# Second layer's latent keys: copy of the values, scaling of the keys and fetch of two weights, moved

## Chip, cores and metric

One Trainium2 chip, one core. The metric is the device time of one launch in microseconds (us). Before the change it was 4139.23 us, median of 3 runs (4138.19 to 4139.9).

## What is computed

The reference is a chain of two blocks over 1024 tokens of width 1024: a hybrid layer (multiscale pooling, an RWKV-7 scan, a mixture of experts) and then two attention layers, the first with grouped queries, the second with latent keys and values ("MLA"). All is float32. The change touches the second attention layer alone, and there the building of keys and values:

```python
MLA_HEADS = 16; MLA_NOPE = 64; MLA_ROPE = 32; MLA_V = 64; MLA_Q_LORA = 384; MLA_KV_LORA = 256

def kv_heads(kv_a, k_r, n):
    kv = (rms_norm(kv_a, p["kv_a_norm"]) @ p["w_kv_b"]).reshape(B, n, MLA_HEADS, MLA_NOPE + MLA_V)
    k_nope, v = jnp.split(kv, [MLA_NOPE], axis=-1)
    return rms_norm(k_nope, p["k_nope_norm"]), rms_norm(k_r, p["k_rope_norm"]), v
...
kn_all = jnp.concatenate([kc_nope, k_nope], axis=1)   # 256 context + 1024 tokens
v_all = jnp.concatenate([vc, v], axis=1)
o = sweep_query_blocks(lambda qn, qr: mla_attend(qn, qr, kn_all, kr_all, v_all), q_nope, q_rope)
```

## The kernel before

Every engine has its own instruction stream, written by walking one list of steps: `walk(order, *engines)` calls, for each step in the list, one function per engine (PE, ACT, DVE, POOL, SP), and each of them emits its part of the step with its waits on semaphores. So the order of the steps in the list is the order of the instructions on each engine; an instruction that waits holds up all that stands behind it on its engine.

The tokens are 10 tiles of 128 rows (`NTT` = 10: `CTX` = 2 tiles of context, then 8 of the sequence).

**Latents** (`latents`, L2840 on; its list is `order(i)`). For each tile: the product for the keys' latent (step `kv`, L2896), its RMS norm and scaling, the same for the queries' latent (`qa`, L2905), the gate (`gate`, L2916, 16 matmuls of 128x512, evacuated by ACT's `silu` L2965), and `latturn`, the turning of the scaled latents: 2 transposes for keys (L2923) and 3 for queries (L2930) into banks 6 and 7, copied out by DVE (L2981, into `kvaT`) and ACT (L2945, into `qaT`). The turning of tile i-1 stands behind the product of tile i; the last, `latturn` of tile 9, stood alone behind the list. Two steps of the list are fetches on SP's queue: `weights2` at tile 3 (the gate row and four blocks of the output weights, L3063 and L3065) and `weights3` at tile 9, which waits for the last product, turning and evacuations and then fetches the first half of the key and value weights (`sp_load_wk`, L2830, 1024 KB into `wkb`) and of the query weights (`sp_load_wq`, L2834, 1152 KB into `wqb`).

**Keys** (`keys(hh)`, L3133, run for each half `hh` of the 16 heads, 8 heads at a time). For each tile c:

- `key` (L3166): 4 matmuls of 128x512 give keys and values of 8 heads in two banks: 0 and 1 for even c, 2 and 3 for odd c. It waits for the weights, for `kvaT`, and for these banks to be free. In the trace each of these float32 matmuls is two records, so a `key` is "x8".
- `ksquare` (L3244, ACT): squares of the keys, from PSUM. `ksum` (L3297 reduce and L1821 mean on DVE, then the root, L1825, on POOL).
- `kscale`: DVE multiplies the keys by the root (L3306, the one that reads PSUM) and then by the norm's weight (L3309); POOL copies the rotary part beside them (L3373).
- `vcopy` (L3251, ACT): copies the values out of PSUM. It frees the two banks for the `key` of tile c+2.
- `kturn` (L3177): 8 transposes of the scaled keys into banks 4 and 6, copied into `kT` by DVE (L3291, four heads) and ACT (L3236, four heads).

The list, for tile c: `key(c)`, `kturn(c-2)` with both copies, `kscale(c-1)`, `vcopy(c-1)`, `ksquare(c)`, `ksum(c)`, then three slots for the queries of the first block (`mmq` L3187 with its copy `qe` L3316 into and out of bank 5, then `qsquare`, `qsum`, `qscale`, `qnorm`, `qadd`). `vcopy(c-1)` waits for L3306 of the same tile (the token `t["ksrc"]`). After the loop come `kturn(8)`, `kscale(9)`, the first turning of the queries (L3196) and `kturn(9)`; then the attention of this half begins with the scores (L3225).

Of the kernel before, what the change touches and what calls it, by code (L numbers as in the profile page):

```python
# [1804 lines left out]
NTT = CTX + NT  # L1805
# [1032 lines left out]
def latents(k, a, dr, m, mod):  # L2838
# [21 lines left out]
    def order(i):  # L2860

        yield ("kv", i)
        if i:
            yield ("latturn", i - 1)
        yield from (("kvsquare", i), ("kvscale", i), ("krsquare", i), ("krscale", i))
        if i >= CTX:
            yield from (("qa", i), ("kradd", i), ("qasquare", i), ("qascale", i))
        if i and i + 1 < NTT:
            yield ("turn", i + 1)
        if i + 3 < NTT:  # L2870
            yield ("load", i + 3)
        if i and i + 2 < NTT:
            yield from (("square", i + 2), ("mean", i + 2), ("divide", i + 2))
        if i == 3:
            yield ("weights2",)
        if i >= CTX:
            yield ("gate", i)
            if i == NTT - 1:
                yield ("weights3",)
            yield ("silu", i)  # L2880
# [87 lines left out]
    def dve_latents(kind, i=None):  # L2968
# [10 lines left out]
        elif kind == "latturn":  # L2979
            dve.wait_ge(*t["kvturn"])  # L2980
            dve.e.tensor_copy(kvaT[:, :, P * i:P * i + P], k.bank(6)[:, 0:256].rearrange("p (k t) -> p k t", k=2)).then_inc(*evac_v.up())  # L2981
            t["kva"] = free[6] = evac_v.at
        elif kind == "kvsquare":
# [59 lines left out]
    def sp_latents(kind, i=None):  # L3043
# [17 lines left out]
        elif kind == "weights2":  # L3061
            sp.wait_ge(*product.at)
            sp.e.dma_start(m.gate, dr["mod"][1, 0, 2 * D:3 * D].partition_broadcast(P)).then_inc(*m.gates_in.up(16))  # L3063
            for kk in range(4):
                sp.e.dma_start(m.wo[kk], m.wo_v[kk]).then_inc(*m.o_in.up(16))  # L3065
        elif kind == "weights3":
            for tok in (product.at, feed.turned.at, feed.squared.at, feed.t["v", NTT - 1], feed.t["a", NTT - 1]):
                sp.wait_ge(*tok)
            t["wk", 0] = m.sp_load_wk(0)
# [6 lines left out]
def mla(k, a, dr, out, m, programs):  # L3076
# [11 lines left out]
    for i in range(CTX, NTT):  # L3088
        walk(m.order(i), *programs)
    walk([("latturn", NTT - 1)], *programs)  # L3090


# [45 lines left out]
    def keys(hh):  # L3138
        bg = queries(hh, 0)
        for c in range(NTT):  # L3140
            yield ("key", hh, c)
            if c > 1:
                yield ("kturn", c - 2)
            if c:
                yield from (("kscale", c - 1), ("vcopy", c - 1))
            yield from (("ksquare", c), ("ksum", c))
            for _ in range(3):
# [3 lines left out]
        yield ("kturn", NTT - 2)  # L3151
        yield from (("kscale", NTT - 1), ("vcopy", NTT - 1))
        yield from (s for s in bg if s)
        yield from (s for s in q_turn(hh, 0, 0) if s)
        yield ("kturn", NTT - 1)

    def pe_program(kind, *x):
        if kind == "key":
            hh, c = x
            pe.wait_ge(*t["wk", hh])  # L3160
            pe.wait_ge(*t["kva"])
            for half in range(2):
# [67 lines left out]
    def act_program(kind, *x):  # L3230
        if kind == "kturn":
            c = x[0]
# [13 lines left out]
        elif kind == "vcopy":  # L3246
            c = x[0]
            act.wait_ge(*t["ksrc"])
            for tok in t["kT free"]:
                act.wait_ge(*tok)  # L3250
            act.e.activation(V[:, c, :].rearrange("p (h d) -> p h d", h=8), key_source(c)[:, :, 64:128], ACT.Copy).then_inc(*evac_a.up())  # L3251
            t["v"] = free[2 * (c % 2)] = free[2 * (c % 2) + 1] = evac_a.at
        elif kind == "qTe" and x[2]:
# [31 lines left out]
    def dve_program(kind, *x):  # L3285
        if kind == "kturn":
            c = x[0]
# [13 lines left out]
        elif kind == "kscale":  # L3301
            c = x[0]
            dst, r8_ = k8s[c % 2][:, :, 0:64], mx[:, 8 * (c % 2):8 * (c % 2) + 8]
            dve.wait_ge(*t["kroot", c])
            dve.wait_ge(*t["kfree", c % 2])
            dve.e.tensor_tensor(dst, key_source(c)[:, :, 0:64], bc(r8_, 2, 64), ALU.mult).then_inc(*keyed.up())  # L3306
            t["ksrc"] = keyed.at
            dve.wait_ge(*keyed.at)
# [275 lines left out]
```

## Time and profile before

| | |
|---|---|
| median of 3 runs | 4139.23 us (4138.19 to 4139.9) |
| profiled execution | 4141.4 us, its span 4139.7 us |
| mean granted clock of TensorE | 0.965 of full speed |
| PE busy | 3769.9 us (91%) |
| DVE, ACT, POOL busy | 1604.3 us (39%), 1216.1 us (29%), 525.6 us (13%) |
| share of the chain that ended last | PE 78%, DVE 9%, issue 5%, ACT 3%, POOL 2%, DMA 2% |
| L3166 (keys), share of that chain | 2% |

Times in the rows are us from the start of the span. The chain that ended last is followed back from the last instruction; what stands in it is what the end waited for. Matmuls overlap their weight loads and one another, so the duration of one record is longer than the distance to the next.

### The profile page before, as it was taken

What the parts mean: (1) busy time and instruction counts of PE and PEld (TensorE: products, weight loads), DVE (VectorE), ACT (ScalarE), POOL (GpSimd) and SP (SyncE); (2) the same over time, 40 slices, a digit from 0 to 9 for tenths busy, and PEclk for the clock granted to TensorE, in tenths of its full rate; (3) what the DMA queues carried; (4) which work ended last, traced back from release to release, by engine and by line L of the source; (5) the groups of instructions that cost most, each with busy time, mean ns of one, the idle gap of its engine ahead of it and who ended that gap; (6) DMA issues with size and microseconds to landing.
All of it is one profiled execution on the core that took longest, in us unless ns stands there. A gap on an engine that the chain in (4) does not pass through costs nothing.

```text
span 4139.7 us, 56854 instructions
## 1 busy us (share of the span) xinstructions
PE 3769.9 (91%) x24715; PEld 2347.9 (57%) x24715; DVE 1604.3 (39%) x2422; ACT 1216.1 (29%) x2101; POOL 525.6 (13%) x499
## 2 busy tenths in 40 slices
PE   8899999989799999988998988888997999889989
PEld 4466666665477776344555555555553666456654
DVE  2444444443311111823444444443223444444430
ACT  1333323310111111523333333332112444344430
POOL 0211212111000000411100100010112000200001
PEclk9999999999799999999999999998999999999999
DMA  3000000212699999920000000020100000000002
GB/s 105 16 17 22 17 17 12 84 37 102 247 366 365 368 366 337 380 56 16 16 11 6 16 16 16 11 88 28 51 11 32 1 1 12 1 1 1 1 31 72
DMA packets 108048, 346.80 MB, mean 84 GB/s; under 512 B 13350, under 2 KB 39270, under 8 KB 89622
## 3 DMA queue, kind: packets, MB, share of 16 engines
q1 hardware_dynamic: 85862, 284.85, 19.0%
q0 software_dynamic: 9072, 33.03, 2.3%
q10 hardware_dynamic: 12864, 25.27, 1.7%
q8 instruction: 195, 3.19, 0.3%
q14 instruction: 55, 0.45, 0.0%
HBM read 296.94 MB, written 46.19 MB: 83 GB/s over the span
## 4 chain that ended last, share of the span: by engine, by line
PE 78%; DVE 9%; issue 5%; ACT 3%; POOL 2%; DMA 2%; SPq 0%; POOLq 0%; ACTq 0%; DVEq 0%
PE ps L2522 10%; PE ps L1613 8%; PE ps L2018 8%; PE ps L383 7%; PE ps L3225 6%; PE ps L2540 4%; PE ps L2045 4%; PE ps L1630 4%; PE ps L2916 3%; PE ps L1207 3%; DVE sb L1992 2%; PE ps L3166 2%; PE ps L3187 2%; PE ps L457 2%; PE ps L468 1%
## 5 line engine op out<-in xcount | busy, mean ns | idle before, releaser
L2522 PE MATMUL ps<-sb 128*128 128x512 f32 x960 | 472.8, 610 | 55.4 <-DVE sb L2682 22.1
L2018 PEld LDWEIGHTS ps<-sb 128*128 128x128 f32 x2624 | 300.5, 145 | 341.1 <-ACT sb L2026 130.8
L2026 ACT ACTIVATE sb<-ps 128x512 f32<-128x512 f32 x400 | 238.8, 597 | 799.7 <-PE ps L2018 799.7
L2018 PE MATMUL ps<-sb 128*128 128x128 f32 x2624 | 430.1, 288 | 47.7 <-ACT sb L2002 18.5
L2002 ACT ACTIVATE sb<-ps,sb 128x1280 f32<-128x1280 f32 (+1 forms) x288 | 352.1, 1230 | 143.9 <-DVE sb L1995 141.0
L383 PE MATMUL ps<-sb 128*128 128x512 f32 x704 | 356.5, 622 | 5.0 <-DMA sb<-in_w_in 3.4
L1613 PE MATMUL ps<-sb 128*128 128x256 f32 x1504 | 341.6, 380 | 0.8 <-ACT sb L1645 0.8
L3225 PE MATMUL ps<-sb 96*128 96x512 f32 (+1 forms) x768 | 339.5, 536 | 0.0
L2033 DVE COPY sb<-ps 128x512 f32<-128x512 f32 x256 | 177.0, 692 | 413.5 <-PE ps L2018 413.2
L2045 PEld LDWEIGHTS ps<-sb 128*64 128x64 f32 x5248 | 290.2, 139 | 72.5 <-ACT sb L2026 37.0
L2045 PE MATMUL ps<-sb 128*64 128x128 f32 x5248 | 325.7, 279 | 2.9 <-DVE sb L2033 1.6
L1613 PEld LDWEIGHTS ps<-sb 128*128 128x128 f32 x1504 | 283.3, 191 | 57.1 <-issue 22.7
L1992 DVE TENSOR_REDUCE sb<-ps 128x1 f32<-128x1024 f32 (+1 forms) x192 | 200.6, 1046 | 235.3 <-PE ps L3225 231.3
L1983 DVE TENSOR_REDUCE sb<-ps 128x2 f32<-128x2560 f32 (+1 forms) x80 | 191.8, 2398 | 231.9 <-PE ps L2540 231.9
L1825 POOL TENSOR_TENSOR sb<-sb 128x1 f32<-128x1 f32 (+3 forms) x114 | 132.7, 1166 | 1153.4 <-DVE sb L1821 1153.3
L2522 PEld LDWEIGHTS ps<-sb 128*128 128x128 f32 x960 | 163.9, 194 | 174.9 <-issue 105.9
L2540 PE MATMUL ps<-sb 64*128 64x256 f32 (+1 forms) x832 | 183.5, 573 | 4.5 <-ACT sb L2002 2.7
L383 PEld LDWEIGHTS ps<-sb 128*128 128x128 f32 x704 | 120.5, 192 | 107.3 <-issue 99.4
L1630 PE MATMUL ps<-sb 128*128 128x512 f32 x376 | 169.5, 593 | 0.0
L2540 PEld LDWEIGHTS ps<-sb 64*128 64x128 f32 x832 | 104.5, 204 | 105.5 <-issue 94.3
L3225 PEld LDWEIGHTS ps<-sb 96*128 96x128 f32 x768 | 124.4, 195 | 14.3 <-issue 11.5
L961 POOL TENSOR_TENSOR sb<-sb 128x512 f32<-128x512 f32 x72 | 92.3, 1289 | 297.2 <-ACT sb L645 126.5
(361 smaller groups left out, 4677.9 us busy)
## 6 DMA issues: line engine op xcount, KB each, us to landing
sb<-in_exp_gate SPq DMA_DIRECT2D x47, 1024.0 KB
sb<-in_exp_up SPq DMA_DIRECT2D x47, 1024.0 KB
sb<-in_exp_down SPq DMA_DIRECT2D x47, 1024.0 KB
sb<-in_l_w_mod ACTq DMA_DIRECT2D x12, 2048.0 KB
d_ys<-sb SPq DMA_DIRECT2D x47, 512.0 KB, 14.1
sb<-d_x SPq DMA_DIRECT2D x32, 512.0 KB, 4.1
sb<-in_w_in SPq DMA_DIRECT2D x22, 512.0 KB, 4.2
sb<-in_x SPq DMA_DIRECT2D x16, 512.0 KB, 5.0
```

Of the source, the lines that this page charges most:

```text
L383: ins = pe.e.matmul(k.bank(6 + half), wt[i % 2][:, kk, :], xT[:, kk, half_of(half)], start=kk == 0, stop=kk == 7)
L1613: ins = pe.e.matmul(k.bank(bank)[:, 0:256], xT[s][:, kk, :], ww[:, 256 * kk:256 * kk + 256], start=kk == 0, stop=kk == 7)
L1630: ins = pe.e.matmul(k.bank(5 + half), hT[s][:, j, :], dw[w][:, 1024 * j + 512 * half:1024 * j + 512 * half + 512], start=j == 0, stop=j == 1)
L1983: dve.e.tensor_reduce(self.mx[:, i:i + 2], src, AX, ALU.min).then_inc(*self.maxed.up())
L1992: dve.e.tensor_reduce(out, src, AX, ALU.min).then_inc(*self.maxed.up())
L2002: act.e.activation(self.Pb[g % 2][:, self.cols(g, b)], self.k.ps[:, self.cols(g, b)], ACT.Exp, bias=self.mx[:, i:i + 1], scale=-1.0, accum ...
L2018: ins = k.pe.e.transpose(k.bank(6)[:, 128 * j:128 * j + 128], self.Pb[g % 2][:, 1280 * b + 128 * c:1280 * b + 128 * c + 128], k.f(C_ID, 128))
L2026: k.act.e.activation(self.PT[:, xs[0]:xs[-1] + 1, :], k.bank(6)[:, 0:128 * len(xs)].rearrange("p (j t) -> p j t", j=len(xs)), ACT.Copy).th ...
L2045: ins = k.pe.e.matmul(k.bank(7)[64 * b:64 * b + 64, o:o + 128], values(c, b), self.PT[:, nk * b + c, :], start=c == 0, stop=c == nk - 1, s ...
L2522: ins = pe.e.matmul(k.bank(5), lhs[:, kk, :], w[:, kk, 512 * half:512 * half + 512], start=kk == 0, stop=kk == 7)
L2540: ins = pe.e.matmul(k.ps[:, 1280 * b + lo:1280 * b + hi], qT[hs, aa, j, :], kT[hs, aa, lo:hi], start=True, stop=True, skip_group_check=True)
L3225: ins = pe.e.matmul(k.ps[:, 1280 * b + lo:1280 * b + hi], qT[0:96, h, :], kT[:, h, lo:hi], start=True, stop=True, skip_group_check=True)
```

## The change

Four things move; no arithmetic is added or taken away.

1. `vcopy(c)` moves from behind `kscale(c)` to directly behind `ksquare(c)`. It no longer waits for L3306. The two banks are now freed by L3306 (`free[...] = keyed.at`), which in turn waits for the copy of the values.
2. `kturn` is split: the transposes on PE keep their place, and the two copies become a step `kTe(c-2)` behind `kscale(c-1)`.
3. `latturn(9)` goes behind the first `key`. `key` waits for the copy of its own tile's latent (`t["kva", c]`) and not for the last.
4. `weights3` is gone; both weights are fetched in `weights2`, at tile 3, behind the output weights on the same queue and with no wait of their own.

```diff
@@ order(i), pe/dve/sp_latents
             yield ("gate", i)
-            if i == NTT - 1:
-                yield ("weights3",)
             yield ("silu", i)
...
-            t["kva"] = free[6] = evac_v.at
+            t["kva", i] = free[6] = evac_v.at
...
                 sp.e.dma_start(m.wo[kk], m.wo_v[kk]).then_inc(*m.o_in.up(16))
-        elif kind == "weights3":
-            for tok in (product.at, feed.turned.at, feed.squared.at, feed.t["v", NTT - 1], feed.t["a", NTT - 1]):
-                sp.wait_ge(*tok)
             t["wk", 0] = m.sp_load_wk(0)
             t["wq", 0] = m.sp_load_wq(0)
...
-    walk([("latturn", NTT - 1)], *programs)
@@ keys(hh)
             yield ("key", hh, c)
+            if hh == c == 0:
+                yield ("latturn", NTT - 1)
             if c > 1:
                 yield ("kturn", c - 2)
             if c:
-                yield from (("kscale", c - 1), ("vcopy", c - 1))
-            yield from (("ksquare", c), ("ksum", c))
+                yield ("kscale", c - 1)
+            if c > 1:
+                yield ("kTe", c - 2)
+            yield from (("ksquare", c), ("vcopy", c), ("ksum", c))
...
         yield ("kturn", NTT - 2)
-        yield from (("kscale", NTT - 1), ("vcopy", NTT - 1))
+        yield ("kscale", NTT - 1)
+        yield ("kTe", NTT - 2)
...
         yield ("kturn", NTT - 1)
+        yield ("kTe", NTT - 1)
@@ act_program, vcopy
-            act.wait_ge(*t["ksrc"])
...
-            t["v"] = free[2 * (c % 2)] = free[2 * (c % 2) + 1] = evac_a.at
+            t["v"] = evac_a.at
@@ dve_program, kscale
             dve.wait_ge(*t["kfree", c % 2])
+            dve.wait_ge(*t["v"])
             dve.e.tensor_tensor(dst, key_source(c)[:, :, 0:64], bc(r8_, 2, 64), ALU.mult).then_inc(*keyed.up())
-            t["ksrc"] = keyed.at
+            free[2 * (c % 2)] = free[2 * (c % 2) + 1] = keyed.at
```

How the instructions stand on three engines. In the changed kernel the lines have other numbers: L3167 is `key` (before L3166), L3178 `kturn` (L3177), L3188 `mmq` (L3187), L2921 and L2928 `latturn` (L2923, L2930), L3311 and L3314 `kscale` (L3306, L3309), L3295 and L3239 the copies of `kturn` (L3291, L3236), L3301 the reduce (L3297), L3247 `ksquare` (L3244), L3253 `vcopy` (L3251), L3321 the copy of `mmq` (L3316).

TensorE from the last gate of the latents to the second key tile of the first half, before (`wo_in6` is the semaphore of the key weights, `wo_in7` that of the query weights):

```order
L2916 MATMUL ps<-sb 128x512 x15
L2923 MATMUL ps<-sb 128x128 [waits evac_v,dve_out]
L2930 MATMUL ps<-sb 128x128 [waits evac_a,dve_out]
L3166 MATMUL ps<-sb 128x512 [waits evac_v,wo_in6]
L3187 MATMUL ps<-sb 128x512 [waits evac_a,wo_in7]
L3166 MATMUL ps<-sb 128x512 [waits gated]
```

and after the change:

```order
L2914 MATMUL ps<-sb 128x512 x15
L3167 MATMUL ps<-sb 128x512 [waits dve_out,wo_in6]
L2921 MATMUL ps<-sb 128x128 [waits evac_v]
L2928 MATMUL ps<-sb 128x128 [waits evac_a,dve_out]
L3188 MATMUL ps<-sb 128x512 [waits evac_a,wo_in7]
L3167 MATMUL ps<-sb 128x512 [waits gated]
```

The first key tile now stands ahead of the last turning of the latents; the first product of the queries still stands behind that turning and waits for its copy (`evac_a`).

VectorE, one inner key tile (the first half, tile 6), before:

```order
L3291 COPY sb<-ps 96x4x128 [waits turned]
L3306 TENSOR_TENSOR sb<-ps,sb 128x8x64 [waits scan_p]
L3309 TENSOR_TENSOR sb<-sb 128x8x64 [waits scan_v]
L3297 TENSOR_REDUCE sb<-sb 128x8 [waits act_out]
L1821 TENSOR_SCALAR sb<-sb 128x8 [waits scan_v]
```

and after the change:

```order
L3311 TENSOR_TENSOR sb<-ps,sb 128x8x64 [waits evac_a,turned,scan_p]
L3314 TENSOR_TENSOR sb<-sb 128x8x64 [waits scan_v]
L3295 COPY sb<-ps 96x4x128 [waits turned]
L3301 TENSOR_REDUCE sb<-sb 128x8 [waits act_out]
L1821 TENSOR_SCALAR sb<-sb 128x8 [waits scan_v]
```

The copy of the turned keys went from ahead of the two scalings to behind them.

ScalarE, the same tile, before:

```order
L3236 ACTIVATE sb<-ps 96x4x128 [waits turned]
L3251 ACTIVATE sb<-ps 128x512 [waits scan_v]
L3244 ACTIVATE sb<-ps 128x512 [waits scan_mm]
```

and after the change:

```order
L3239 ACTIVATE sb<-ps 96x4x128 [waits turned]
L3247 ACTIVATE sb<-ps 128x512 [waits scan_v,scan_mm]
L3253 ACTIVATE sb<-ps 128x512
```

The copy of the values now follows the square with no wait of its own, and the copy of the turned keys is still ahead of the square.

## Rows read from the trace of the kernel before

**Rows 1.** Chain that ended last: start us, us, engine and line; fetch, then one tile
```profile
3116.14 6.03 DMA sb<-in_l_w_kv_b
...
3148.08 0.45 PE ps L3177 x4
...
3148.55 0.69 DVE sb L3291
...
3149.88 0.61 ACT sb L3251
```

**Rows 2.** Timeline of PE, first half: start, length, instruction, [idle before, releaser]
```profile
3115.95 0.38 PE L2923 MATMUL ps<-sb 128*128 128x128 f32 x2
...
3122.21 5.29 PE L3166 MATMUL ps<-sb 128*128 128x512 f32 x8 [5.55 <-DMA sb<-in_l_w_kv_b]
3127.34 2.73 PE L3187 MATMUL ps<-sb 128*128 128x512 f32 x6
3129.91 3.60 PE L3166 MATMUL ps<-sb 128*128 128x512 f32 x8
3135.72 2.08 PE L3187 MATMUL ps<-sb 128*128 128x256 f32 x4 [2.21 <-DVE sb L3316]
...
3144.38 3.70 PE L3166 MATMUL ps<-sb 128*128 128x512 f32 x8 [1.14 <-ACT sb L3251]
...
3150.53 3.70 PE L3166 MATMUL ps<-sb 128*128 128x512 f32 x8 [1.57 <-ACT sb L3251]
...
3191.98 1.08 PE L3177 MATMUL ps<-sb 128*96 128x128 f32 x8 [2.98 <-DVE sb L3309]
...
3194.69 5.67 PE L3225 MATMUL ps<-sb 96*128 96x512 f32 x12
```

**Rows 3.** Timeline of PE, second half of the heads
```profile
3578.91 1.62 PE L3187 MATMUL ps<-sb 128*128 128x256 f32 x4 [2.21 <-DVE sb L3316]
...
3637.58 6.09 PE L3225 MATMUL ps<-sb 96*128 96x512 f32 x12
```

**Rows 4.** Timeline of DVE, an inner tile and the last one
```profile
3149.16 0.68 DVE L3306 TENSOR_TENSOR sb<-ps,sb 128x512 f32<-128x512 f32 x1
...
3150.99 0.69 DVE L3297 TENSOR_REDUCE sb<-sb 128x8 f32<-128x512 f32 x1 [0.42 <-ACT sb L3244]
3151.72 0.17 DVE L1821 TENSOR_SCALAR sb<-sb 128x8 f32<-128x8 f32 x1
...
3188.58 0.17 DVE L1821 TENSOR_SCALAR sb<-sb 128x8 f32<-128x8 f32 x1
...
3190.50 0.69 DVE L3306 TENSOR_TENSOR sb<-ps,sb 128x512 f32<-128x512 f32 x1 [1.17 <-POOL sb L1825]
3191.23 0.69 DVE L3309 TENSOR_TENSOR sb<-sb 128x512 f32<-128x512 f32 x1
3191.84 0.68 DVE L3281 COPY sb<-ps 96x512 f32<-96x512 f32 x1
```

**Rows 5.** Timeline of ACT, the same inner tile
```profile
3148.99 0.59 ACT L3236 ACTIVATE sb<-ps 96x512 f32<-96x512 f32 x1 [2.04 <-PE ps L3177]
...
3150.37 0.59 ACT L3244 ACTIVATE sb<-ps 128x512 f32<-128x512 f32 x1
```

**Rows 6.** Timeline of POOL: the root beside the queries' scaling, and alone
```profile
3158.11 2.28 POOL L1825 TENSOR_TENSOR sb<-sb 128x8 f32<-128x8 f32 x1 [2.56 <-DVE sb L1821]
...
3170.40 1.64 POOL L1825 TENSOR_TENSOR sb<-sb 128x8 f32<-128x8 f32 x1 [4.05 <-DVE sb L1821]
```

**Rows 7.** SP's queue: issues of the next three x tiles after the fetches at tile 3
```profile
2982.24 48.80 SPq L1880 DMA_DIRECT2D sb<-d_x  x3
```

**Rows 8.** Windows: stretch, length, busy PE, PEld, DVE, ACT, POOL, granted clock, DMA share, GB/s
```profile
2958.00:2974.00 16.00, 16.00 (x43) 7.82 (x42) 3.27 (x8) 3.56 (x7) 1.10 (x2) 1.00 0.56 198
2974.00:2982.00 8.00, 8.00 (x36) 5.48 (x35) 2.53 (x11) 1.63 (x6) 1.50 (x4) 1.00 0.00 0
...
3122.20:3127.50 5.30, 5.29 (x9) 2.43 (x10) 0.00 (x0) 0.00 (x0) 0.00 (x0) 0.69 0.34 138
```

More of the change, by code:

```diff
@@ L3155, in keys @@
         yield ("kturn", NTT - 1)
+        yield ("kTe", NTT - 1)
     def pe_program(kind, *x):
-        if kind == "key":
+        if kind == "latturn":
+            programs[0](kind, *x)
+        elif kind == "key":
             hh, c = x
             pe.wait_ge(*t["wk", hh])
-            pe.wait_ge(*t["kva"])
+            pe.wait_ge(*t["kva", c])
             for half in range(2):
@@ L3230, in act_program @@
     def act_program(kind, *x):
-        if kind == "kturn":
+        if kind == "latturn":
+            programs[1](kind, *x)
+        elif kind == "kTe":
             c = x[0]
@@ L3285, in dve_program @@
     def dve_program(kind, *x):
-        if kind == "kturn":
+        if kind == "latturn":
+            programs[2](kind, *x)
+        elif kind == "kTe":
             c = x[0]
```

## The prediction

> **What bounds the kernel now.** I read the page first. PE is 91% busy and 78% of the chain that ended last, so what can be won is where the chain leaves PE. I then read that chain in order of time over the stretch that the change touches, from the last latents to the first scores. It leaves PE in two places. The first is the fetch of the key weights: 6.03 us of DMA that nothing covers [rows 1]. PE's timeline shows the hole, 5.55 us of idle, and right behind it a `key` of 5.29 us where the next takes 3.60 [rows 2]; the granted clock of that stretch is 0.69, so part of it ran at 1.2 GHz after the idle time [rows 8]. The second recurs in every key tile: `key` 3.70 us on PE, half of the turning 0.45, its copy on DVE (the next starts after 3149.16 - 3148.55 = 0.61), the scaling L3306 until ACT starts 0.72 (3149.88 - 3149.16), and the copy of the values on ACT 0.61; only then are the banks free and PE, idle for 1.57 us, goes on [rows 1, 2, 4]. From one `key` to the next it is 3150.53 - 3144.38 = 6.15 us [rows 2]. I then read DVE, ACT and POOL for the distances inside such a tile [rows 4 to 6], and last the queue and the DMA share at the place to which the fetch moves [rows 7, 8].
>
> **Part 1, the fetch and the last turning.** The fetch leaves the joint, so the first `key` follows the last gate directly, where now the turning stands: 3115.95 [rows 2]. PE has been busy without a break, so I take 3.70 us at full clock: end 3119.65. The turning, moved behind it, has 5 transposes at 0.11 us each, to 3120.2. New is a wait: the first product of the queries needs ACT's copy of this turning (about 0.5 us, an estimate between the 0.59 of rows 5 and the shorter tile of 384 elements; bounds 0 and the 2.21 us that a copy on DVE held PE up [rows 2]). So the six records of `mmq` start at 3120.75 and take 3129.91 - 3127.34 = 2.57, the second `key` starts at 3123.3, ends 3.60 later, and the 2.21 us until DVE has read bank 5 stay as they are [rows 2]: the second part of `mmq` starts at 3129.13. Before, it is 3135.72 [rows 2]. **Gain 6.6 us**, of which 1.6 is clock (5.29 - 3.70). If the clock fell here all the same, 5.0; if there were no new wait, 7.1.
>
> The fetch itself goes to tile 3, on a queue that then has 2.6 MB of its own. The DMA share is 0.56 in the 16 us from 2958 and 0.00 in the 8 us behind [rows 8]. The first of the two weights, 1024 KB, lands 6.03 us after its issue [rows 1]; at that rate the added 2176 KB take 13 us, at the worst. The next load of an x tile is issued at 2982.24 and the three that remain are 24 us apart (48.80 for two steps), a latent tile each [rows 7]; such a tile is squared a latent tile after its load. I cost the fetch at nothing; without that cover, an x tile would be late by some of the 13 us.
>
> **Part 2, the period of a key tile.** The banks are now freed by L3306, the copy of the values is off the path, and the copy of the turned keys is behind the scaling. What is late next? Two rings remain, and PE's own work.
>
> - *DVE and POOL.* L3306 to L3309 0.73; to the next on DVE, now the copy of the turned keys, 0.61; from that copy to the next, now the reduce, 0.61 as well; reduce to mean 0.73; mean to L3306, through POOL's root, 1.92 [rows 1, 4]. Sum 4.60 us, one ring per tile.
> - *Through PE and ACT, once in two tiles.* `key` 3.70; both halves of the turning 0.91 (3148.99 - 3148.08); ACT's copy to its next 0.49 (3150.37 - 3149.88); square to reduce 0.62 (3150.99 - 3150.37); reduce to mean 0.73; mean to L3306 1.92; L3306 to PE 0.75, as from L3309 to PE (3191.98 - 3191.23). Sum 9.1, so 4.56 a tile [rows 1, 2, 4, 5].
> - *PE alone.* 8 records of 0.43 (2.57 / 6) and 8 transposes of 0.11 (0.45 / 4): 4.3 us.
>
> So the period falls from 6.15 to about 4.6, and DVE is what is late. In the tile in which DVE scales the queries beside the root, the root takes 2.28 instead of 1.64 [rows 6]. Before it was covered; now it is in the ring: +0.6, once in each half of the heads.
>
> The walk from the second part of `mmq` (A): before, `key` 3 starts at A+8.66 with 1.14 of idle [rows 2]; that idle goes, since its banks were freed long ago: A+7.5. From `key` 3 to `key` 9 six steps: 4.4 (PE's), 4.7, 5.2 (with the +0.6), 4.7, 4.6, 4.6 = 28.2, before 6 x 6.15 = 36.9. The tail: before, 13.4 from `key` 9 (3144.38 + 36.9 = 3181.28) to the scores (3194.69). After, L3306 of tile 9 comes two rings behind that of tile 7, which is 0.75 ahead of `key` 9: +8.45; L3309 +0.73; the copy of tile 8, which now stands between L3309 and the last turning, +0.61; the turning +0.75; the scores 2.71 behind it [rows 2]: 13.25. So this copy gives back 0.6 us that the ring has won. Scores at A+48.95.
>
> Before it is 3194.69 - 3135.72 = 58.97 in the first half and 3637.58 - 3578.91 = 58.67 in the second [rows 2, 3]. **Gain 10.0 and 9.7 us.**
>
> PE's idle time ahead of the last turning grows from 2.98 us [rows 2] to about 3.9. The clock may fall earlier there; the price of a fall is bounded by 0 and the 1.6 us of rows 2, in each half. I take 0, since the first scores are slow before too: 12 records take 5.67 and 6.09 us [rows 2, 3], at 0.43 each they would take 5.3.
>
> **Sum.** 6.6 + 10.0 + 9.7 = 26.3 us. The profiled execution took 4141.4 us (span 4139.7); it lies 2.2 above the median of the runs, 4139.23, from which I take the gain: **4112.9 us**. Own range of this case: +3.2 (clock), +2.2 (the new wait), -0.5, -1.2 (the root not longer): 4109 to 4118.
>
> **A rule against it.** The root is in the ring now, so its length counts in every tile. Alone it takes 1.64 us, beside two DVE instructions of 768 elements 2.28 [rows 6]. The order of the change leaves DVE with nothing to do while the root runs, but for the queries' steps, so I count the longer one once. The Trainium skill, "GPSIMD Engine Reference", Key points, says that GpSimd shares its SBUF interfaces with VectorE and suffers from VectorE instructions with two SBUF inputs; L3309 is one. By that rule the moved order, which packs DVE's work closer to POOL's, might lengthen every root.
>
> **Rivals.**
> 1. *Every root is long* (8%): 2.28 in each ring makes the period 5.24. That is 0.64 more in some 7 rings in each half, 8 or 9 us less gain: 4121. For it: the 2.28 of rows 6. Against: in the ring DVE waits for the root by its own order. It is the outcome that the skill's rule above would give.
> 2. *PE is the bound* (6%): if the rings run shorter than their sums (they are only 0.3 above PE's 4.3), the period is 4.3: 0.3 x 12 = 3.6 us more, 4109.
> 3. *Only the fetch pays* (4%): the change doesn't do in the loop what it says. If L3306 is held by one of its three waits (values, turning, root) until where the old order had it, the period stays near 6.15 and 6.6 us are left: 4132.6. Against: the values are copied 0.5 us behind the square, far ahead of the root.
> 4. *Slower* (2%): the early fetch holds up the x tiles. Place: the load at 2982.24. It decides from the point where the queue is not empty by then and the tile lands over 24 us late; to outweigh 26 us of gain three tiles would have to wait some 12 us each, 36 us: 4149. Against: the DMA share of 0.00 from 2974 to 2982, 8 us in which nothing moves [rows 8].
>
> **Chances.** 80% for the forecast, 8, 6, 4 and 2% for the rivals. The range that should hold the time 8 times in 10 is the forecast's own, stretched to rivals 1 and 2: 4108 to 4121. A measurement of this kernel can tell about 0.2%, 8.3 us, from no change: forecast and rivals 1 and 2 are faster by more (94%), rival 3 is within it (4%), rival 4 slower (2%).
>
> **What would show it.** Right: no wait of PE for the key weights, and the first `key` at 3.7 us; L3167 to L3167 4.6 us in the inner tiles, PE's idle time in them 0.3 us and ended by L3311 on DVE; one longer tile in each half; 3.9 us of idle ahead of the last turning; the scores 26 us earlier in the second half. Wrong: a root of 2.3 us in all tiles; idle PE among the latents from 2982 on; slow `key`s in the middle of the loop; a gain that the attention gives back.

## The result, and the profile after

| | before | after |
|---|---|---|
| median | 4139.56 us, 6 runs (4138.19 to 4141.4) | 4111.11 us, 6 runs (4110.79 to 4114.03) |
| span of the profiled execution | 4139.7 us | 4111.2 us |
| mean granted clock | 0.965 | 0.965 |
| PE busy | 3769.9 us (91%) | 3764.8 us (92%) |
| DVE, ACT, POOL busy | 1604.3, 1216.1, 525.6 us | 1603.5, 1214.8, 527.4 us |
| share of the chain that ended last | PE 78%, DVE 9%, ACT 3%, POOL 2% | PE 77%, DVE 10%, ACT 3%, POOL 3% |

The ratio is 0.9933, with an interval of 0.992 to 0.9945: 28.4 us less, where 26.3 were forecast. In a later series the same kernel took 4112.02 us beside 4140.11 of before. No engine does less work worth the name; PE waits less.

I cut both profiled executions at the same four instructions: the first turning behind the last gate (in the changed kernel the first `key` stands there), the first scores of the first half, the first `key` of the second half, its first scores.

| stretch, us | before | after | gain |
|---|---|---|---|
| start to last gate | 3115.95 | 3116.24 | -0.29 |
| A: joint and keys, first half | 78.74 | 61.13 | 17.61 |
| B: attention, first half | 372.41 | 371.71 | 0.70 |
| C: keys, second half | 70.48 | 58.79 | 11.69 |
| D: attention, second half, to the end | 502.12 | 503.33 | -1.21 |
| sum | 4139.7 | 4111.2 | 28.5 |

All of the gain lies in A and C, where the change is. The attention, six times as long as A and C before the change, gives back half a microsecond on balance.

Two of these stretches scatter in code that no edit touches, but for the fetch at tile 3: over the 13 profiled executions of this case the last gate is reached between 3112.33 us (z3) and 3118.93 us (y1), and D takes 500.5 to 504.3 us. So A and C are what the traces can be compared by.

PE's timeline of the changed kernel, first half, from the first `key` to the scores (start, length, instruction, idle time before it and what ended it):

```profile
3116.24 3.60 PE L3167 MATMUL ps<-sb 128*128 128x512 f32 x8
...
3121.06 2.81 PE L3188 MATMUL ps<-sb 128*128 128x512 f32 x6 [0.67 <-ACT sb L2943]
...
3129.52 1.13 PE L3188 MATMUL ps<-sb 128*128 128x256 f32 x4 [2.21 <-DVE sb L3321]
3130.49 3.60 PE L3167 MATMUL ps<-sb 128*128 128x512 f32 x8
...
3135.23 3.60 PE L3167 MATMUL ps<-sb 128*128 128x512 f32 x8
...
3144.24 3.70 PE L3167 MATMUL ps<-sb 128*128 128x512 f32 x8 [0.16 <-DVE sb L3311]
...
3149.45 3.70 PE L3167 MATMUL ps<-sb 128*128 128x512 f32 x8 [0.63 <-DVE sb L3311]
...
3154.13 3.70 PE L3167 MATMUL ps<-sb 128*128 128x512 f32 x8
...
3158.70 3.70 PE L3167 MATMUL ps<-sb 128*128 128x512 f32 x8
...
3163.28 3.70 PE L3167 MATMUL ps<-sb 128*128 128x512 f32 x8
...
3169.26 1.05 PE L3178 MATMUL ps<-sb 128*96 128x128 f32 x8 [1.41 <-DVE sb L3295]
...
3173.83 1.91 PE L3178 MATMUL ps<-sb 128*96 128x128 f32 x8 [3.08 <-DVE sb L3295]
...
3177.37 5.92 PE L3226 MATMUL ps<-sb 96*128 96x512 f32 x12
```

Against [rows 2]: the DMA wait of 5.55 us is gone; in its place stands one of 0.67 us for ACT's copy of the last turning. The first `key` is 3.60 us long, not 5.29. The 2.21 us ended by the copy out of bank 5 are still there, in the second half too. The rows at 3135.23 and 3163.28 are `key` 3 and `key` 9. The inner `key`s are 3158.70 - 3154.13 = 4.57 us apart, where it was 6.15, and PE shows no wait of note ahead of them; the one at 3149.45 is the tile with the queries' scaling. Ahead of the last turning PE is idle for 3.08 us.

DVE, from one L3311 to the next in an inner tile:

```profile
3157.95 0.69 DVE L3311 TENSOR_TENSOR sb<-ps,sb 128x512 f32<-128x512 f32 x1 [1.76 <-POOL sb L1825]
3158.68 0.69 DVE L3314 TENSOR_TENSOR sb<-sb 128x512 f32<-128x512 f32 x1
3159.29 0.68 DVE L3295 COPY sb<-ps 96x512 f32<-96x512 f32 x1
3159.89 0.67 DVE L3301 TENSOR_REDUCE sb<-sb 128x8 f32<-128x512 f32 x1
3160.60 0.17 DVE L1821 TENSOR_SCALAR sb<-sb 128x8 f32<-128x8 f32 x1
3162.53 0.69 DVE L3311 TENSOR_TENSOR sb<-ps,sb 128x512 f32<-128x512 f32 x1 [1.76 <-POOL sb L1825]
```

This is the ring of the prediction, DVE's five instructions and POOL's root: 0.73 + 0.61 + 0.60 + 0.71 + 1.93 = 4.58 us. DVE waits only for the root; the 0.42 us for the square of [rows 4] are gone. The ring, not PE, sets the pace, though the idle time that PE shows in such a tile is nearly nothing; y2 and y4 below test this.

POOL, the root of the queries' tile and of an inner tile:

```profile
3146.39 2.28 POOL L1825 TENSOR_TENSOR sb<-sb 128x8 f32<-128x8 f32 x1 [0.98 <-DVE sb L1821]
...
3160.85 1.64 POOL L1825 TENSOR_TENSOR sb<-sb 128x8 f32<-128x8 f32 x1 [2.58 <-DVE sb L1821]
```

One root of 2.28 us in each half, beside the two multiplications of 768 elements, and the next of 1.75, beside two of 256 elements; the others take 1.64 or 1.65, as [rows 6].

SP's queue at latent tile 3, and the windows of [rows 8] there (stretch, length, busy PE, PEld, DVE, ACT, POOL, granted clock, DMA share, GB/s):

```profile
2961.12 0.48 SPq L2830 DMA_DIRECT2D sb<-in_l_w_kv_b  x1
2961.64 0.63 SPq L2834 DMA_DIRECT2D sb<-in_l_w_q_b  x1
2982.51 0.34 SPq L1880 DMA_DIRECT2D sb<-d_x  x1
```

```profile
2958.00:2974.00 16.00, 16.00 (x44) 7.88 (x43) 3.42 (x9) 3.57 (x7) 1.10 (x2) 1.00 0.87 335
2974.00:2982.00 8.00, 8.00 (x35) 5.41 (x34) 2.51 (x10) 1.43 (x5) 1.51 (x4) 1.00 0.01 4
```

The DMA share of the 16 us rises from 0.56 to 0.87, and almost nothing is left on the queue by 2974 (0.01). The next x tile is issued at 2982.51; in the kernel before it was 2982.24 [rows 7]. PE is busy all through both stretches.

### The profile page after: what moved, and what is told of

It reads as the page before. It is cut to its first block, busy times and chain, and to the rows that moved or that the text cites. A ratio compares the mean times of both kernels' runs of the same rounds, so it can differ in the third digit from the quotient of the medians.

```text
span 4111.2 us, 56888 instructions
## 1 busy us (share of the span) xinstructions
PE 3764.8 (92%) x24715; PEld 2348.1 (57%) x24715; DVE 1603.5 (39%) x2422; ACT 1214.8 (30%) x2101; POOL 527.4 (13%) x499
## 4 chain that ended last, share of the span: by engine, by line
PE 77%; DVE 10%; issue 5%; ACT 3%; POOL 3%; DMA 2%; SPq 1%; POOLq 0%; ACTq 0%; DVEq 0%
PE ps L2522 10%; PE ps L2018 8%; PE ps L1613 7%; PE ps L383 7%; PE ps L3226 6%; PE ps L2540 4%; PE ps L2045 4%; PE ps L1630 4%; PE ps L2914 3%; PE ps L1207 3%; DVE sb L1992 2%; PE ps L457 2%; PE ps L3188 2%; POOL sb L1825 2%; PE ps L468 1%
## 5 line engine op out<-in xcount | busy, mean ns | idle before, releaser
L2045 PEld LDWEIGHTS ps<-sb 128*64 128x64 f32 x5248 | 290.1, 139 | 72.4 <-ACT sb L2026 37.0
L2045 PE MATMUL ps<-sb 128*64 128x128 f32 x5248 | 325.6, 279 | 2.9 <-DVE sb L2033 1.6
```

Source lines behind the costliest of these rows:

```text
L2045: ins = k.pe.e.matmul(k.bank(7)[64 * b:64 * b + 64, o:o + 128], values(c, b), self.PT[:, nk * b + c, :], start=c == 0, stop=c == nk - 1, s ...
```

## The experiments

Eleven runs of ten kernels. "Changed" is the kernel after the change. Each time is a median beside the kernel before in the same series (4140.74 us for the four named x, 4140.19 for the four named y, 4140.11 for the three named z). For each I also cut the profiled execution as above.

| kernel | median, us | ratio to before | interval | A, us | C, us |
|---|---|---|---|---|---|
| before | 4140 to 4141 | | | 78.74 | 70.48 |
| x2, fetch alone | 4133.34 | 0.9983 | 0.9974 to 0.9992 | 71.87 | 70.48 |
| x1, fetch and turning | 4131.82 | 0.9979 | 0.997 to 0.9988 | 71.45 | 69.13 |
| y1, loop alone | 4122.80 | 0.9954 | 0.994 to 0.9968 | 68.22 | 58.79 |
| x3, keys' copies not moved | 4122.95 | 0.996 | 0.9946 to 0.9973 | 65.66 | 65.91 |
| x4, values' copy not moved | 4119.81 | 0.995 | 0.9936 to 0.9964 | 63.33 | 62.30 |
| y4, longer roots | 4118.66 | 0.9951 | 0.9937 to 0.9965 | 64.28 | 64.58 |
| z1, changed | 4112.02 | 0.9934 | 0.992 to 0.9947 | 61.11 | 58.81 |
| z2, bank 5 read earlier | 4106.44 | 0.992 | 0.9906 to 0.9933 | 57.49 | 56.83 |
| y2, keys' copies last | 4102.59 | 0.9907 | 0.9892 to 0.9922 | 56.56 | 55.58 |
| y3, all of it | 4094.91 | 0.9893 | 0.9878 to 0.9908 | 53.65 | 52.20 |
| z3, the same kernel | 4094.65 | 0.9892 | 0.9877 to 0.9907 | 53.64 | 52.19 |

**x1 and x2: the joint.** x2 is the kernel before with the fetch at tile 3 and nothing else; x1 moves the last turning too, and leaves the loop as it was.

```diff
 x2, against before
-            if i == NTT - 1:
-                yield ("weights3",)
...
-        elif kind == "weights3":
-            for tok in (product.at, feed.turned.at, feed.squared.at, feed.t["v", NTT - 1], feed.t["a", NTT - 1]):
-                sp.wait_ge(*tok)
 x1, beside that
-    walk([("latturn", NTT - 1)], *programs)
...
             yield ("key", hh, c)
+            if hh == c == 0:
+                yield ("latturn", NTT - 1)
...
-            pe.wait_ge(*t["kva"])
+            pe.wait_ge(*t["kva", c])
```

> Kernel before with parts 3 and 4 of the change alone: weights fetched at tile 3, last turning behind the first key. My theory: the joint and the loop are separate and add up. PE no longer waits 5.55 us for the fetch, the first key takes 3.6 us and not 5.29, PE waits some 0.7 us for the copy of the turning: gain 6.5 us, about 4133; the key tiles keep their 6.15 us. Rival: the early fetch helps the loop too or costs among the latents: then the gain is not between 5 and 8.

> Kernel before with part 4 alone: the fetch at tile 3, the last turning left ahead of the first key. My theory: the fetch is all of the joint's gain. The first key waits for DVE's copy of the latent, 0.2 to 0.5 us, and the queries' product for nothing, so the time is within 0.5 us of that with part 3 as well, gain 6.5 to 7, about 4132.5. Rival: the turning's place matters, because the idle time at the joint lets the clock fall: then 1.5 us or more slower than with part 3.

Measured: 8.9 us less than before for x1 and 7.4 for x2. Both rivals' conditions were met, if narrowly: the gain of x1 is not between 5 and 8, and x2 is 1.5 us slower than x1. The loop is not where it comes from: x1's own keys behind the joint are 6.15 us apart, as before. Its A and C together are 8.6 us shorter than before, 6.5 of it at the joint, the rest where the clock stayed up (below). PE's timeline of x2, and behind it two rows of x1:

```profile
3115.65 0.38 PE L2921 MATMUL ps<-sb 128*128 128x128 f32 x2
...
3116.64 3.67 PE L3161 MATMUL ps<-sb 128*128 128x512 f32 x8 [0.28 <-DVE sb L2979]
3120.15 2.74 PE L3182 MATMUL ps<-sb 128*128 128x512 f32 x6
...
3128.53 2.08 PE L3182 MATMUL ps<-sb 128*128 128x256 f32 x4 [2.21 <-DVE sb L3311]
3130.40 4.37 PE L3161 MATMUL ps<-sb 128*128 128x512 f32 x8
```

```profile
3129.58 1.13 PE L3185 MATMUL ps<-sb 128*128 128x256 f32 x4 [2.21 <-DVE sb L3318]
3130.54 3.60 PE L3164 MATMUL ps<-sb 128*128 128x512 f32 x8
```

With the turning left ahead of the first `key`, PE waits 0.28 us for DVE's copy and not at all for ACT's, which is done while the `key` runs. From the first turning to the second part of `mmq` x2 takes 3128.53 - 3115.65 = 12.88 us, x1 13.28 (3129.58 - 3116.30), before 19.77. So as far as waits go, the fetch alone is the whole gain of the joint: moving the turning swaps a wait of 0.28 us for one of 0.67 and costs 0.4 us.

The last rows hold something else. In x2 the clock falls behind the idle 2.21 us, as before (4.37 us for the `key` of tile 2; the `mmq` ahead of it takes 2.08 us as in [rows 2]); in x1 it doesn't, in either half. From the second part of `mmq` to `key` 3 x1 takes 7.00 us and x2 8.68 in the first half; at the end of the loop x1 loses 0.9 us of that again, since there its last turning is the slow one (1.94 us for 1.08). The 1.5 us between the medians is of that size, but the runs of the two kernels overlap (4128.3 to 4134.1, 4131.3 to 4136.2), so whether the turning's place is worth something through the clock stays open. More on this at the end.

**x3 and x4: the two moves in the loop, each without the other.** Both keep the joint of the changed kernel. In x3 the values are copied behind the square and the banks are freed by L3310 (the changed kernel's L3311), but the copies of the turned keys stay ahead of the scaling. In x4 those copies move, but the values are still copied behind the scaling, wait for it and free the banks.

```diff
 x3, against changed
             if c > 1:
                 yield ("kturn", c - 2)
+                yield ("kTe", c - 2)
             if c:
                 yield ("kscale", c - 1)
-            if c > 1:
-                yield ("kTe", c - 2)
...
         yield ("kturn", NTT - 2)
+        yield ("kTe", NTT - 2)
         yield ("kscale", NTT - 1)
-        yield ("kTe", NTT - 2)
 x4, against changed
             if c:
-                yield ("kscale", c - 1)
+                yield from (("kscale", c - 1), ("vcopy", c - 1))
             if c > 1:
                 yield ("kTe", c - 2)
-            yield from (("ksquare", c), ("vcopy", c), ("ksum", c))
+            yield from (("ksquare", c), ("ksum", c))
...
```

> The changed kernel with part 2 undone: the copies of the turned keys are back ahead of the scaling; values still behind the square, banks still freed by the scaling. My theory: the period is key 3.70, half turning 0.45, copy 0.61, scaling 0.75: 5.5 us, ended by DVE. That keeps only 0.6 of the 1.57 us that a tile gained: some 12 us less gain than the change, 4123. Rival: taking the values off the path is all that pays: 4111 and 4.6 us a tile.

> The changed kernel with part 1 undone: values copied behind the scaling, and they free the banks, copies of the turned keys still behind the scaling. My theory: the ring through PE and ACT gets longer by the copy of the values, 9.74 us in two tiles, 4.87 a tile against 4.57: 3 to 4 us slower than the change, 4114.7. Rival: PE has slack for the later bank, the DVE and POOL ring alone sets the pace: no difference, 4111.

x3 came out as expected, 4122.95 us. Its `key`s:

```profile
3139.72 3.70 PE L3166 MATMUL ps<-sb 128*128 128x512 f32 x8 [0.94 <-DVE sb L3310]
...
3145.23 3.70 PE L3166 MATMUL ps<-sb 128*128 128x512 f32 x8 [0.94 <-DVE sb L3310]
```

They are 5.51 us apart: of the 6.15 us before, the values' copy was 0.6, and the scaling in front of it now ends the wait.

x4 missed: 4119.81 us for an expected 4114.7. The chain that ended last in x4, one inner tile (start, length, engine and line):

```profile
3156.37 0.70 DVE sb L3311
...
3157.09 0.60 ACT sb L3254
3157.69 0.48 ACT sb L3239
3158.17 0.50 ACT sb L3247
...
3158.69 0.70 DVE sb L3302
...
3159.41 0.18 DVE sb L1821
...
3159.66 1.65 POOL sb L1825
...
3161.33 0.70 DVE sb L3311
```

There is another ring, through ACT, that I had not summed. The copy of the values (L3254) waits for L3311, and on ACT's queue the copy of the turned keys (L3239) and the square (L3247) stand behind it; the reduce waits for the square. That makes 3161.33 - 3156.37 = 4.96 us a tile, 0.4 more than with the values copied behind the square. So the move of the values does two things: it takes a copy out of PE's wait for its banks, and it clears ACT's queue ahead of the square. Each move alone leaves a longer ring than the two together: 5.51 and 4.96 against 4.57.

**y1: the loop alone.** The changed kernel with fetch and last turning put back.

```diff
 y1, against changed
             yield ("gate", i)
+            if i == NTT - 1:
+                yield ("weights3",)
...
             yield ("key", hh, c)
-            if hh == c == 0:
-                yield ("latturn", NTT - 1)
...
```

> Kernel before with parts 1 and 2 alone: fetch and last turning where they were. My theory: the loop's gain stands by itself, period 4.57 us, PE waits 5.55 us for the fetch and the first key is slow again: gain 28.4 - 6.5 = 22, some 4117.6. Rival: the gains overlap: then the two parts measured alone add up to more than the change.

The median is 4122.80 us, 5 over what was expected, in runs that spread from 4112.38 to 4125.61. The trace of the execution says where it isn't: A and C are 10.5 and 11.7 us shorter than before, 22.2 in all, as expected. It reached the last gate at 3118.93 us, 3 us later than before and in code that y1 does not touch, and D took 504.0, 1.9 us more than before. So the loop's gain is shown in A and C of one execution; the median is 5 us short of it, in stretches that scatter by that much without an edit, and can't be split closer. By medians the parts add up to 8.9 + 17.4 = 26.3 us for 28.4 of the whole.

**y2: the copies of the turned keys behind the sums.** If the ring through DVE and POOL is the bound, the copy L3295 (0.61 us in it) can leave it by standing where DVE waits for the root anyway. Then PE's 4.31 us a tile are the bound.

```diff
 y2, against changed
             if c:
                 yield ("kscale", c - 1)
-            if c > 1:
-                yield ("kTe", c - 2)
             yield from (("ksquare", c), ("vcopy", c), ("ksum", c))
+            if c > 1:
+                yield ("kTe", c - 2)
```

> The changed kernel with the copies of the turned keys one step later still, behind square, values and sum of the tile. My theory: they leave both rings: DVE and POOL 4.57 - 0.61 = 3.96 us, through PE and ACT 7.75 in two tiles; PE is the bound, 4.3 us a tile. 0.27 us in some 5 tiles of each half: 2 to 3 us faster than the change, 4108.5, PE idle under 0.1 us in the inner tiles. Rival: PE was the bound already (it idled 0.31 at most): no difference.

Measured 4102.59 us, 6 less than expected. PE's timeline of y2, two inner `key`s, the last turning and the scores:

```profile
3153.69 3.60 PE L3167 MATMUL ps<-sb 128*128 128x512 f32 x8
...
3158.00 3.60 PE L3167 MATMUL ps<-sb 128*128 128x512 f32 x8
...
3171.39 1.05 PE L3178 MATMUL ps<-sb 128*96 128x128 f32 x8 [1.70 <-DVE sb L3295]
...
3173.66 4.46 PE L3226 MATMUL ps<-sb 96*128 96x512 f32 x12
```

The period is 4.31 us, so the ring was the bound, by 0.27 us a tile, and PE is now. In the second half the six steps from `key` 3 to `key` 9 take 26.23 us instead of 28.04: 1.8 gained. (This alone doesn't tell the two rings apart, since the copy leaves both; y4 does.) What my expectation left out is the tail. In the changed kernel DVE's ring lags behind PE by the end of the loop; without the lag the last scaling comes 6.91 us behind `key` 9 and not 8.4, PE's idle time ahead of the last turning is 1.69 us and not 3.08, and the scores start 11.61 us behind that `key`, not 13.23 (all of the second half). In the first half the tail is shorter by 2.7 us, of which some 1.1 is clock (last turning 1.05 us for 1.91). A and C together are 7.8 us shorter than in the changed kernel. So a lag of a ring is paid twice: per tile, and once more where the loop drains.

**y4: longer roots.** This kernel adds two multiplications of 768 elements from a buffer in SBUF into an unused place of it, on DVE, behind the mean of tiles 3 and 5 to 8, beside the root. They add nothing to the result.

```diff
 y4, against changed
             t["kmean"] = keyed.at
+            if 3 <= c < NTT - 1 and c != 4:
+                for _ in range(2):
+                    dve.e.tensor_tensor(Pb[1][:, 1024:1792], Pb[1][:, 1792:2560], Pb[1][:, 1792:2560], ALU.mult).then_inc(*keyed.up())
+                    dve.wait_ge(*keyed.at)
```

> The changed kernel with two more DVE multiplications of 768 elements (both inputs in SBUF, into an unused buffer) behind the mean of tiles 3 and 5 to 8 of each half, beside POOL's root; 10 roots in all. They take 2.0 us and the root with its waits 1.92, so by themselves they add 0.1 us a tile, 1 us in all: 4112. My theory: beside them the root takes 2.28 us and not 1.64, and all of that is in the ring: 5.2 us a tile in these tiles, 6 us slower, 4117. Rival (the ring through PE or PE itself sets the pace): under 3 us slower.

Measured 4118.66 us. POOL's timeline of y4, and PE's:

```profile
3160.98 2.28 POOL L1825 TENSOR_TENSOR sb<-sb 128x8 f32<-128x8 f32 x1 [2.64 <-DVE sb L1821]
...
3171.50 1.64 POOL L1825 TENSOR_TENSOR sb<-sb 128x8 f32<-128x8 f32 x1 [2.64 <-DVE sb L1821]
```

```profile
3158.83 3.70 PE L3167 MATMUL ps<-sb 128*128 128x512 f32 x8 [0.69 <-DVE sb L3315]
...
3164.09 3.70 PE L3167 MATMUL ps<-sb 128*128 128x512 f32 x8 [0.69 <-DVE sb L3315]
```

The roots of those tiles take 2.28 us, the one of tile 9, which has no extra work beside it, 1.64. The `key`s are 5.26 us apart, the 5.24 that rival 1 worked out, and PE shows the wait that it did not show at 4.57. The root is 0.64 us longer and the step 0.69. The root counts once per tile, then; in the ring through PE and ACT, which takes two tiles, it would have added 0.3 us a tile. So the root is in the ring of DVE and POOL. The median is not all the root's, though: in two steps of each half DVE has the queries' work besides, does not wait for the root, and the added multiplications themselves lengthen the step (5.93 us for 4.71, and 5.71 for 4.68). That is 2.25 of the 3.64 us that the six steps gain in length, so that 4118.66 lies near the expected 4117 is in part luck. The Trainium skill, "GPSIMD Engine Reference", Key points, says that GpSimd suffers from VectorE instructions with two SBUF inputs; the 2.28 us agree. So does y2, where the copy L3295, whose one input is in PSUM, runs beside the inner roots and they stay at 1.64. In the changed kernel it doesn't bite because L3314, the one such instruction of the ring, is over before the root starts (3159.37 against 3160.85).

**z1 and z2: the 2.21 us behind the first `mmq`.** z1 is the changed kernel again. In z2 the queries' slot of tile 1, in which DVE reads bank 5, stands ahead of the square and the sum and not behind.

```diff
 z2, against changed
+            if c == 1:
+                yield from slots(bg)
             yield from (("ksquare", c), ("vcopy", c), ("ksum", c))
...
-            for _ in range(3):
+            for _ in range(2 if c == 1 else 3):
                 yield from slots(bg)
```

> The changed kernel itself, beside the others on one chip: 28 us faster than before. In its trace the third key of each half starts behind 2.21 us of idle PE. If the clock's fall there is chance, it will be 3.6 us in one half and longer in another, or differ from the first trace of this kernel; if the change had cured it, 3.6 us in both halves again.

> The changed kernel with one move: at tile 1 of each half DVE reads bank 5 (the queries' product) ahead of the sum of tile 1. My theory: PE loses no 2.21 us there, twice, 4.4 us faster than the changed kernel, and no clock falls there. Rival: the rings start later by as much, since the sum of tile 1 is 0.6 us later: under 2 us faster.

z1 took 4112.02 us, 28.1 less than before. The `key` behind the idle 2.21 us took 3.60 us in both halves again, which is what I had written for a cure; but y4 and x3, which have the same order there, show 5.29 us for that `key` in their second half, so the change is no cure.

z2 took 4106.44 us, 5.6 less than z1 for 4.4 expected. Its row at that place has no wait:

```profile
3126.25 1.03 PE L3190 MATMUL ps<-sb 128*128 128x256 f32 x4
```

So those 2.21 us, which before and after share, are the order of DVE's work and not the product; from `key` 1 to `key` 2 z2 takes 4.30 us where z1 takes 6.78, in both halves. A is 3.6 us shorter and C 2.0; what differs from 2.5 is mostly clock at the last turning (1.05 us for 1.91 in the first half, 1.57 for 1.05 in the second).

**y3 and z3: the three together.** y2 and z2, and in the tail the copy of the eighth turned tile back ahead of `kscale(9)`. y3 and z3 are one kernel in two series.

```diff
 y3 and z3, against changed, beside the edits of y2 and z2
         yield ("kturn", NTT - 2)
-        yield ("kscale", NTT - 1)
         yield ("kTe", NTT - 2)
+        yield ("kscale", NTT - 1)
```

> The same, and two more moves: in the tail the copies of tile 8 ahead of the scaling of tile 9 (0.6 us in each half), and bank 5 of the queries' product read ahead of the sum of tile 1 (2.21 us of idle PE in each half). My theory: 2.5 + 1.2 + 4.4 = 8 us faster than the change, 4103. Rival: the idle time only moves to the third key, which then waits for the scaling of the first: 4.4 us less, 4107.5.

> The fastest version of the call before again, on one chip with the changed kernel: 14 to 16 us faster than the changed kernel, 43 to 45 us faster than before.

The medians are 4094.91 and 4094.65 us, the second 17.4 less than z1 in the same series. The first expectation, 4103, missed by 8 us: it had taken 2.5 us for the copies (y2 is 8.5 us below the changed kernel) and 4.4 for bank 5 (z2: 5.6). The second, 14 to 16 us, was exceeded by 1.4. PE's timeline of z3:

```profile
3163.67 1.08 PE L3180 MATMUL ps<-sb 128*96 128x128 f32 x8 [1.23 <-DVE sb L3316]
...
3165.97 4.46 PE L3228 MATMUL ps<-sb 96*128 96x512 f32 x12
...
3174.31 1.92 PE L3228 MATMUL ps<-sb 96*128 96x512 f32 x2
```

PE sets the pace (inner `key`s are 4.31 us apart), the tail has 1.23 us of idle time, and the first scores run without a slow record. In the first half the slow records only come later: behind PE's next idle time, 2.96 us, two records of L3228 take 1.92 us, where two take 1.02 at full clock. From the first scores to L2045, the next product of the attention with the values, it is 21.47 us in z3 and 21.45 in the changed kernel, so there the fast scores won nothing; in the second half it is 19.99 for 21.25. This kernel beats both, by 45 us against before (ratio 0.9892, interval 0.9877 to 0.9907).

## Why the prediction was right, and where it was off

The mechanism held: an uncovered fetch, and a period that two waits in series had set. 4112.9 us were forecast, 4111.11 measured. Step by step, in the order of the prediction:

- **The joint (6.6 us): 6.5.** From the first instruction behind the last gate to the second part of `mmq`: 13.28 us for 19.77. The new wait for ACT's copy was costed at about 0.5 us and is 0.67. What the prediction did not say is that part 3 of the change has no share in this: x2 has all of it without moving the turning. Whether part 3 helps through the clock behind the 2.21 us is open.
- **The fetch at tile 3 at nothing: right.** The weights landed 11.7 and 14.1 us after their issue, so by 2976, and the x tiles kept their times (three issues over 48.81 us, before 48.80). Rival 4 is dead.
- **From the second part of `mmq` to `key` 3: 5.71 us, taken as 7.5. This is the term that was mis-sized.** I took away the 1.14 us of idle ahead of that `key` and left the clock as it had been. But the `mmq` of 2.08 and 1.62 us in [rows 2, 3], and the `key` of tile 2 behind it, 4.35 and 4.84 us in the same trace, ran partly at the lower clock; in the changed kernel they took 1.13 and 3.60 us, in both halves, in both profiled executions of it. That is 1.8 us in each half that the forecast hadn't, 1.7 of it in these two records. It is partly luck: the forecast had no reason for the clock to stay up here, and in y4 and x3, with the same order, it fell in the second half.
- **Six steps from `key` 3 to `key` 9 (28.2 us): 28.05 and 28.04.** Inner steps 4.57 or 4.58 us (4.6), the queries' tile 3149.45 - 3144.24 = 5.21 (5.2), with a root of 2.28 us. The ring was named right, and y4 and y2 show that it is one: a root longer by 0.64 us lengthens the step by 0.69, and taking the copy out shortens it to PE's own 4.31. The sign that I had named for it, 0.3 us of idle PE ended by L3311 in the inner tiles, does not stand in the timeline; it shows only at 3144.24 (0.16) and in the queries' tile (0.63).
- **The tail (13.25 us): 13.23 in the second half, 14.09 in the first.** In the first half the last turning took 1.91 us and not 1.05: here the clock did fall behind the idle time. The price of 0 that I chose was a little low, well inside the 1.6 us bound. The idle time was 3.08 us and not 3.9, since the turning ahead of it waits as well (1.41 us, ended by L3295) and so starts later; the place of the last turning did not change by that.
- **The 12 score records "at 0.43 each", 5.3 us: wrong.** Only 8 of the 12 are 512 wide; 4 are 256 wide, which the merged row doesn't show. At full clock they take 4.46 us together (y3, z3, the first half of y2), so the first scores of before and after, at 5.67 to 6.09 us, carry 1.2 to 1.6 us of slow clock in each half. It was the argument for costing nothing at that place; the argument holds by another number, since the cost is there in both kernels and cancels in the difference.
- **The range's lower end does not follow from its terms.** 4112.9 less 0.5 and 1.2 is 4111.2, not 4109. The measured 4111.11 lies at that edge. In the profiled executions it is the clock, which the range had only as a cost, that accounts for it. The new wait's bound, 2.21 us, of which about 0.5 was in the sum already, adds 1.7 and not 2.2.
- **Rival 1 (long roots)** did not come: one root of 2.28 us in each half. **Rival 2 (PE is the bound)** did not come: 4.57, not 4.3. y2 is the kernel in which it does. **Rival 3** (only the fetch pays) is x2, at 4133.34 us for the 4132.6 worked out; the changed kernel is 22 us below it.
- **The attention gives nothing back** worth naming: +0.70 and -1.21 us. Over all kernels B lay between 371.5 and 374.5 us and D between 500.5 and 504.3, without regard to the edit.

So the sum was 2.2 us short: 3.6 from the clock behind the two idle 2.21 us and 0.3 from the twelve steps, less 0.8 for the tail of the first half, 0.1 for the joint, and 0.8 for the start and the attention (-0.29 + 0.70 - 1.21), which is inside their scatter. In A and C by themselves it was 3.0 us short (29.3 measured), so the closeness of the total owes something to chance.

In the expectations two rings or tails were missed, and both by the same omission: I followed the edit's own instruction and not what comes behind it (ACT's square on the queue in x4, the drained loop in y2).

## What to carry to other kernels

In a software pipeline over several engines, write down every closed path from a step back to the same step one tile later, each with its sum from start-to-start distances, the ones through a queue's order among them; the longest is the period, and an edit that shortens it wins no more than the distance to the second longest, or to the busiest engine's own work. An engine without idle time of note may still be paced by such a ring, as PE at 4.57 us for work of 4.31. Put a copy that nobody waits for soon where its engine waits for another anyway, and count a ring's lag once more at the end of the loop.

## What was not expected of the hardware

The clock behind one and the same wait. Two windows with the idle 2.21 us and PE's work behind it, first of the kernel before, then of the changed one (the granted clock is the number ahead of the last two); the last row is the last turning of the changed kernel:

```profile
3133.50:3135.70 2.20, 0.01 (x1) 0.00 (x0) 1.46 (x3) 0.60 (x1) 0.55 (x1) 1.00 0.00 0
3135.70:3137.80 2.10, 2.08 (x5) 1.72 (x6) 0.00 (x0) 0.00 (x0) 1.44 (x2) 0.50 0.03 8
```

```profile
3127.30:3129.50 2.20, 0.01 (x1) 0.00 (x0) 1.46 (x3) 1.08 (x2) 0.55 (x1) 1.00 0.00 0
3129.50:3134.00 4.50, 4.48 (x13) 2.39 (x14) 1.39 (x2) 0.00 (x0) 1.44 (x2) 1.00 0.02 4
...
3173.80:3176.50 2.70, 1.91 (x8) 1.47 (x9) 1.17 (x2) 0.59 (x1) 0.00 (x0) 0.50 0.02 6
```

The granted clock is 0.50, the level of 1.2 GHz, behind the wait before the change, and 1.00, 2.4 GHz, behind the same wait after it. Of the 20 such places in ten profiled executions with that wait (two halves each), the clock fell at 7: in both halves of before and x2, in the first of y1, in the second of x3 and y4. It did not in either half of the changed kernel (twice profiled), of x1, x4 and y2, nor in the other halves of y1, x3 and y4. The wait is 2.21 us in all 20, and PE had been busy just ahead of it. In the first half there is a pattern: the clock fell in all three executions with the last turning ahead of the first `key` (before, x2, y1) and in none of the seven with it behind. What PE had done before differs there: in the three it had been idle last for 0.28 us (x2) or 5.3 to 5.6 us (before, y1), ahead of the first `key`; in the seven for 0.67 us, behind it. In the second half, where the two orders are the same, it fell in four of ten: before and x2, but also x3 and y4. x1 and x2 have the same order there and differ. So the turning's place may decide in the first half; what decides in the second is open.

The score records of y2 say the same: 4.46 us in the first half, 5.90 in the second, behind idle times of 1.70 and 1.69 us ahead of the last turning. A fall behind the 2.21 us costs 1.7 us on the spot (6.06 us from the second part of `mmq` to the turning in the first half before, 4.40 in the changed kernel). Part of it comes back: where the clock stayed up there in the first half, in the changed kernel and in x1, the last turning was slow instead, at 0.8 to 0.9 us. The first scores took 1.2 to 1.6 us more than 4.46 in most kernels and 2.0 to 2.8 in x3, x4 and one half of z2 (6.45 to 7.27 us).

The second is how sharply the root answers to DVE: 1.64 us alone, 2.28 us beside two multiplications of 768 elements from SBUF, the same to 0.01 us in the five tiles of each half of y4, in the queries' tile of the changed kernel and in [rows 6]. In those cases the first multiplication began before the root and the second during it. In y2, y3 and z3 the copy stands ahead of the two in the queries' tile, both begin while the root runs, and the root takes 2.87 to 2.88 us. The multiplications take 0.94 to 0.96 us each in either case.
